# Two heads at a time in the dilated part of a decoder trunk's attention, and weight parts dealt differently over the steps

## What is computed

```
h = x @ w_in                       # (256, 3302)
# 4 heads with latent q and kv (q, k of width 96), causal softmax
# 6 forgetting heads (width 64 + 2 columns that carry the log gates), causal softmax
# 6 dilated heads, q and k rotated by position, width 64:
for window, dilation in ((128, 1), (512, 4), (2048, 16)):
    # query t sees t, t-d, ..., t-window; softmax numerators and denominators are summed over the three
    ...
mixed = concat(o_a, o_b, o_c)      # 256 + 384 + 384 = 1024
x = layer_norm(alpha * x + mixed @ w_out)
```

## Time and profile before

| | us |
|---|---|
| median of 3 runs | 868.74 |
| lowest and highest | 868.0, 871.59 |
| the profiled execution: its own time | 867.3 |
| its span, first to last instruction | 865.7 |
| TensorE busy in the span | 816.2 (94%) |
| VectorE busy | 628.9 (73%) |
| ScalarE busy | 503.0 (58%) |
| GpSimd busy | 89.9 (10%) |

### The profile page before, as it was taken

How to read it: one execution, slowest core, us unless ns; L and a number is a source line. 1 busy time by engine, 2 the same in 40 slices (tenths; PEclk the granted TensorE clock), 3 DMA queues, 4 the chain that set the end, 5 groups by cost and what they waited for, 6 DMA issues and landing times.

```text
span 865.7 us, 12257 instructions
## 1 busy us (share of the span) xinstructions
PE 816.2 (94%) x4411; PEld 695.0 (80%) x4411; DVE 628.9 (73%) x1094; ACT 503.0 (58%) x794; POOL 89.9 (10%) x165
## 2 busy tenths in 40 slices
PE   6998899899998999999999989999999989999993
PEld 6997798679876888888889978867898768888882
DVE  4656766775657899999565577666856589999984
ACT  3655554454435788888355646544443467888871
POOL 3156200030000000000020530000200100000001
PEclk9999999999999999999999999999999999999997
DMA  9953353455333699999465524425533439999941
GB/s 275 337 178 111 128 163 106 139 160 190 94 121 121 218 366 370 364 369 372 159 181 166 180 98 146 148 97 195 196 120 100 128 118 306 366 367 366 367 147 49
DMA packets 124110, 177.06 MB, mean 205 GB/s; under 512 B 12320, under 2 KB 92720, under 8 KB 124048
## 3 DMA queue, kind: packets, MB, share of 16 engines
q1 hardware_dynamic: 122064, 169.56, 58.8%
q0 software_dynamic: 1984, 6.70, 2.6%
HBM read 175.18 MB, written 1.05 MB: 204 GB/s over the span
## 4 chain that ended last, share of the span: by engine, by line
PE 81%; DVE 10%; ACT 3%; issue 3%; DMA 1%; POOL 1%; SPq 0%; DVEq 0%; ACTq 0%; POOLq 0%
PE bank L1489 21%; PE bank L1491 21%; PE bank L1490 21%; DVE w_split L490 2%; PE bank L1766 2%; PE bank L1618 2%; PE bank L1659 2%; PE bank L1607 2%; PE bank L1629 1%; PE bank L1596 1%; PE bank L1650 1%; DVE xT_lo L997 1%; DVE p_sb L1046 1%; PE bank L1606 1%; DMA xs<-in_x_dram 1%
## 5 line engine op out<-in xcount | busy, mean ns | idle before, releaser
L490 DVE TENSOR_TENSOR w_split<-raw,w_split 128x1024 fp32r<-128x1024 f32 (+2 forms) x336 | 386.9, 1174 | 74.5 <-ACT w_split L485 69.9
L485 ACT ACTIVATE w_split<-raw 128x1024 fp32r<-128x1024 f32 (+2 forms) x336 | 335.5, 1010 | 111.7 <-PE bank L1491 97.5
L1489 PE MATMUL bank<-w_split,xg_hi 128*128 128x512 f32 x256 | 103.5, 404 | 0.0
L1491 PE MATMUL bank<-w_split,xg_lo 128*128 128x512 f32 x256 | 100.2, 392 | 0.0
L1490 PE MATMUL bank<-w_split,xg_hi 128*128 128x512 f32 x256 | 100.2, 391 | 0.0
L1489 PE MATMUL bank<-w_split,xT_hi 128*128 128x384 f32 (+1 forms) x224 | 77.8, 347 | 2.0 <-DVE w_split L490 1.6
L1491 PE MATMUL bank<-w_split,xT_lo 128*128 128x384 f32 (+1 forms) x224 | 75.7, 338 | 0.0
L1490 PE MATMUL bank<-w_split,xT_hi 128*128 128x384 f32 (+1 forms) x224 | 75.6, 338 | 0.0
L602 POOL TENSOR_SCALAR st<-st 128x1 f32<-128x1 f32 x12 | 5.7, 473 | 653.4 <-ACT junk L748 653.0
L707 ACT ACTIVATE qkT<-bank 66x512 f32<-66x512 f32 (+2 forms) x32 | 19.0, 593 | 80.0 <-PE bank L1596 80.0
L1491 PEld LDWEIGHTS bank<-w_split,xg_lo 128*128 128x128 f32 x256 | 48.1, 188 | 11.0
(11 more groups left out here) (296 smaller groups left out, 1610.0 us busy)
## 6 DMA issues: line engine op xcount, KB each, us to landing
raw<-in_expert_w_gate_dram SPq DMA_DIRECT2D x128, 256.0 KB, 5.0
raw<-in_expert_w_up_dram SPq DMA_DIRECT2D x128, 256.0 KB, 6.7
raw<-in_expert_w_down_dram SPq DMA_DIRECT2D x64, 512.0 KB, 7.0
raw<-in_w_in_dram SPq DMA_DIRECT2D x48, 384.0 KB, 4.2
raw<-in_xattn_w_kv_dram SPq DMA_DIRECT2D x32, 512.0 KB, 3.7
raw<-in_w_mix_out_dram SPq DMA_DIRECT2D x16, 512.0 KB, 4.1
raw<-in_xattn_w_q_dram SPq DMA_DIRECT2D x16, 512.0 KB, 3.4
raw<-in_xattn_w_o_dram SPq DMA_DIRECT2D x16, 512.0 KB, 4.3
```

The source lines that it names most:

```text
L485: nc.scalar.activation(w_hi[:, i % SPL, 0:w], raw[:, i % RAW, 0:w], ACT.Copy).then_inc(hi_ready, 1)
L490: nc.vector.tensor_tensor(w_lo[:, i % SPL, 0:w], raw[:, i % RAW, 0:w], w_hi[:, i % SPL, 0:w].bitcast(F32), ALU.subtract).then_inc(lo_ready, 1)
L1489: nc.tensor.matmul(o, lhs[0], rhs[0], start=first, stop=False, skip_group_check=shared)
L1491: return nc.tensor.matmul(o, lhs[1], rhs[0], start=False, stop=last, skip_group_check=shared)
```

## The change

- Stream and steps: WO1 part 0 changes places with WO0 part 3, so that it comes first after step 18. `slots` deals the 29 parts anew.
- `head_qk` for heads 10, 12 and 14 transposes two heads at once (four 128x128 transposes for both), in steps 10, 12 and 14; the three odd ones fall away. It first waits until VectorE has read the previous head's scores (`s_masked`), as the odd head's scores now go into B_QK.
- `evac_qk` copies both heads with one instruction of 128 rows.
- `head_scores` runs in steps 11, 13 and 15 for two dilated heads: for each of the two token tiles first one head from rows 0 to 63, into B_S, then the other from rows 64 to 127, into B_QK. Steps 12, 14 and 16 have no scores.
- VectorE: both heads' `softmax_max` in the odd step, the first head's `softmax_norm` there too, the second's at the start of the even step. For all other heads `softmax_norm` now stands ahead of `evac_o`.

```diff
-                         ..., ("WO0", range(4)), ("WO1", range(4)),
+                         ..., ("WO0", range(3)), ("WO1", range(1)), ("WO0", range(3, 4)), ("WO1", range(1, 4)),
...
-        slots = [3] + [2] * 2 + [1] * 7 + [2] * 6 + [1] * 3
+        slots = [3, 2, 2] + [2, 1] * 4 + [1, 2] * 2 + [1] * 4
...
+        def in_pair(h):
+            return MLA_H + FOX_H <= h < HEADS
+        def qk_slot(h):
+            return (h // 2 + 1) % 2 if in_pair(h) else h % 2
...
+            return B_QK if (in_pair(h) or h >= HEADS) and (h - HEADS) % 2 else B_S
+        def scored(s):
+            if in_pair(s - 1):
+                return (s - 1, s) if s % 2 else ()
+            return (s - 1,) if 1 <= s <= HEADS else ()
...
-                nc.scalar.activation(qkT[0:d, h % 2, :], B_QK[0:d, :], ACT.Copy).then_inc(qkT_ready.sem, 1)
+                nc.scalar.activation(qkT[0:d, qk_slot(h), :], B_QK[0:d, :], ACT.Copy).then_inc(qkT_ready.sem, n)
...
-                    if 1 <= s <= HEADS:
-                        softmax_max(l, s - 1)
+                    for h in scored(s):
+                        softmax_max(l, h)
+                    if in_pair(s - 1) and s % 2 == 0:
+                        softmax_norm(l, s - 1)
                     if 2 <= s <= HEADS + 1:
                         evac_pT(l, s - 2)
+                    if 1 <= s <= HEADS and not (in_pair(s - 1) and s % 2 == 0):
+                        softmax_norm(l, s - 1)
                     if s >= 3 and (s - 3) % 2 == 1:
...
                         evac_o(l, s - 3)
-                    if 1 <= s <= HEADS:
-                        softmax_norm(l, s - 1)
...
-                if h >= MLA_H + FOX_H:
+                if in_pair(h):
+                    pe.wait_ge(s_masked.sem, s_masked.at(l, 2 * h))
                     pe.nop().then_inc(paused_t, 1)
...
+                        if in_pair(h):
+                            ins = nc.tensor.transpose(B_QK[:, c0:c0 + P], v[:, t, g:g + 2, :].rearrange("p h d -> p (h d)"),
+                                                      ident[:, :])
...
+                if in_pair(h):
+                    pe.wait_ge(qkT_ready.sem, qkT_ready.at(l, h + 2))
+                    pe.wait_ge(s_masked.sem, s_masked.at(l, 2 * h))
+                    for q, k in ((slice(0, P), slice(0, P)), (slice(P, T), slice(P, 3 * P))):
+                        for i in range(2):
+                            v = qkT[i * DIL_D:(i + 1) * DIL_D, qk_slot(h), :]
+                            ins = nc.tensor.matmul(score_bank(h + i)[:, k], v[:, q], v[:, T:T + k.stop - k.start],
+                                                   start=True, stop=True)
+                    ins.then_inc(s_done.sem, 2)
...
-                    if 1 <= s <= HEADS:
-                        head_scores(l, s - 1)
-                    if s < HEADS:
+                    if scored(s):
+                        head_scores(l, scored(s)[0])
+                    if s < HEADS and not (in_pair(s) and s % 2):
                         head_qk(l, s)
-                for i in range(index[l, "WO0", 3], index[l, "MV1", 3]):
+                for i in range(index[l, "WO1", 0], index[l, "MV1", 3]):
                     gemm(i)
```

More of the change, by code:

```diff
@@ L58, in weight_stream @@
                          ("UKV", range(1)), ("FV", range(2, 4)), ("DQ", range(4)), ("DK", range(4)), ("DV", range(4)),
-                         ("MK0", range(4)), ("MK1", range(4)), ("MV0", range(4)), ("WO0", range(4)), ("WO1", range(4)),
+                         ("MK0", range(4)), ("MK1", range(4)), ("MV0", range(4)), ("WO0", range(3)), ("WO1", range(1)), ("WO0", range(3, 4)), ("WO1", range(1, 4)),
                          ("MV1", range(4)), ("XQ0", range(4)), ("XQ1", range(4)), ("XO0", range(4)), ("XO1", range(4)),
@@ L397, in build @@
         feat = lambda w: w.rearrange("(k p) n -> p k n", p=P)
-        slots = [3] + [2] * 2 + [1] * 7 + [2] * 6 + [1] * 3
+        slots = [3, 2, 2] + [2, 1] * 4 + [1, 2] * 2 + [1] * 4
         turns, ahead_of = [], []
         for l in range(L):
-            fill = list(between(l, ("FV", 2), ("WO0", 3)))
+            fill = list(between(l, ("FV", 2), ("WO1", 0)))
             assert sum(slots) == len(fill)
@@ L409, in build @@
             assert len(turns[l]) == HEADS + 3
-            ahead_of.append(turns[l][1:] + [[index[l, "WO0", 3], index[l, "WO1", 0]]])
-        def score_bank(h):
-            return B_QK if h >= HEADS and (h - HEADS) % 2 else B_S
+            ahead_of.append(turns[l][1:] + [[index[l, "WO1", 0], index[l, "WO0", 3]]])
+        def in_pair(h):
+            return MLA_H + FOX_H <= h < HEADS
+        def qk_slot(h):
+            return (h // 2 + 1) % 2 if in_pair(h) else h % 2
+        def score_bank(h):
+            return B_QK if (in_pair(h) or h >= HEADS) and (h - HEADS) % 2 else B_S
[3 more added lines that the diff above has]
+            return (s - 1,) if 1 <= s <= HEADS else ()
         def value_bank(h):
@@ L702, in evac_qk @@
             def evac_qk(l, h):
-                act.wait_ge(qk_done.sem, qk_done.at(l, h + 1))
+                n = 2 if in_pair(h) else 1
+                act.wait_ge(qk_done.sem, qk_done.at(l, h + n))
                 if h >= 2:
                     act.wait_ge(s_done.sem, s_done.at(l, h - 1))
-                d = MLA_D if h < MLA_H else FOX_D if h < MLA_H + FOX_H else DIL_D
-                nc.scalar.activation(qkT[0:d, h % 2, :], B_QK[0:d, :], ACT.Copy).then_inc(qkT_ready.sem, 1)
+                d = MLA_D if h < MLA_H else FOX_D if h < MLA_H + FOX_H else 2 * DIL_D
+                nc.scalar.activation(qkT[0:d, qk_slot(h), :], B_QK[0:d, :], ACT.Copy).then_inc(qkT_ready.sem, n)
             def exps(l, h):
@@ L839, in _ @@
                                     .then_inc(job_a.sem, 1)
-                    if s < HEADS:
+                    if s < HEADS and not (in_pair(s) and s % 2):
                         evac_qk(l, s)
-                    if 1 <= s <= HEADS:
-                        exps(l, s - 1)
+                    for h in scored(s):
+                        exps(l, h)
                     if s >= 3 and (s - 3) % 2 == 1:
@@ L1019, in softmax_max @@
                         sl = slice(0, P) if t == 0 else slice(P, 3 * P)
-                        nc.vector.tensor_tensor_reduce(p_sb[:, h % 2, sl], B_S[:, sl], mask[:, P - P * t:2 * P], scale, -3e38,
+                        nc.vector.tensor_tensor_reduce(p_sb[:, h % 2, sl], score_bank(h)[:, sl], mask[:, P - P * t:2 * P], scale, -3e38,
                                                        ALU.add, ALU.max, mx[:, h, t:t + 1]).then_inc(s_masked.sem, 1)
```

7 lines of the change are left out of this document (4 added, 3 removed).

## The result

The changed kernel takes 845.86 us (median of 4 runs, 845.52 to 846.52), the kernel before in the same comparison 869.18 us (868.0 to 871.59). The ratio is 0.973, with an interval of 0.971 to 0.975: 23.3 us faster. The forecast was 849 us, 844 to 856. The profiled execution took 845.52 us, 21.8 less than the profiled one of before (867.3).

A forecast was written before the change was run, and what follows sets the result against it. TensorE's work and idle moments were taken as the bound. Per layer 4.0 - 1.07 + 5.3 + 1.3 = 9.5 us, 19.0 for two, gave 849.7; with small gaps the forecast was 849 us, range 844 to 856.

The forecast's parts named there:

- What bounds it: Whole kernel: TensorE, busy 94% of the span with 81% of the chain; its own work and its standing still count.
- Part 1: Dilated heads, steps 11 to 16: fewer transposes, paired scores and turns without scores save 4.0 us a layer.
- The assumption of full overlap: Steps 11, 13, 15: two heads' score matmuls run beside each other and cost what one head's do, 1.32 us with the turn.
- the serial rival: Score pairs in steps 11, 13, 15 run one after the other: +0.65 us per pair, 853 us; chance 12%.
- Part 2: Step 10: the transposes wait for head 9's mask, 1.07 us lost per layer.
- Part 3: Steps 3 to 9: five waits for softmax probabilities go, 0.4 us stays in steps 5 and 6; 5.3 us saved a layer.
- Part 4: End of the head steps: 1.5 us of waits stay, 1.5 go; 0.2 lost behind them, 1.3 us a layer net.
- The two small gaps that I left out: Parts starting 0.3 us late where GpSimd rotates, not counted in the terms: worth up to 1 us.
- The waits that come back: Softmax waits return because VectorE, with two parts to split, reaches the mask late: 857 us; chance 10%.
- No change: Head steps: waits only move and the score pairs run serially: 866.7 us; chance 3%.
- The throttle: Dilated steps: pauses bring TensorE's clock from 2.4 to 1.2 GHz, slower, 880 us if over 15 us a layer; chance 3%.

The follow-up runs named there:

- the run with the copy one step later still: Changed kernel without the wait before head 10's transposes, WO0 part 1 split in step 15, MV0's product copied in step 17: 841.52 us.
- the run head by head: Changed kernel with each pair's score matmuls ordered as both token tiles of one head, then both of the other: 846.96 us.

## Why the prediction was right

Point by point, in the terms of its sum, per layer:

- **What bounds it.** TensorE's list, by its work and by the times in which it stands still: right. Behind the head steps the change cost 0.14 us in both layers together, and the experts' stretch only shifted. TensorE's idle time fell by 13.3 us, 11 forecast; 2.1 us of it is the shorter wait for the first DMA, which isn't the change's.
- **Part 1, small work, 4.0 us.** Step 12: 0.74 us, 0.75 forecast. Step 11: 1.37, 1.32 forecast; 0.1 of it is a pause ahead of the next part that steps 13 and 15 (1.28) don't have. Two small errors cancel: the odd steps took 1.65 us before, not step 12's 1.71, so they gave 1.0 us instead of 1.17, and step 16 gave 1.0 instead of 0.93 (a turn alone is 0.30 us without a wait, in the run with the copy one step later still). The busy time fell by 8.5 us, 8.0 forecast. The assumption of full overlap is shown by the run with both heads in one half: 0.65 us more from first to last start, the 0.65 of the serial rival exactly. Its cost on the path was 1.77 us a layer, not 1.95, as it hid the pause of step 11 and 0.1 us of the wait for head 14's turn.
- **Part 2, the wait, 1.07 us lost.** The mechanism was right, the size too small: from the last score's start to the transposes it is 1.77 us in the first layer and 1.50 in the second, where 0.22 is free of a wait, so 1.55 and 1.29, 1.07 forecast. Removing it gives 1.25, as in the first layer 0.3 reappears in a split. Two things were too small. From the end of the mask to the transposes I took 0.05 us, which no row showed; it is 0.27 in both layers (first layer: mask below, transposes at 115.15). And in the first layer the mask itself ends 0.27 us later after the last score than in the kernel before, though GpSimd is idle there; why stays open.

```profile
114.46 0.42 DVE L1035 CUSTOM_DVE_ANT_0 p_sb<-bank,causal 128x256 f32<-128x256 f32 x1
```

- **Part 3, 5.3 us.** The five waits are gone; in the first layer 0.3 stayed in step 4 and 0.1 in step 5, in the second 0.5 in step 3 (forecast: 0.4 in steps 5 and 6). From start to start it is 5.3 us in the first layer.
- **Part 4, 1.5 us less at the end, 0.2 given back.** From start to start 1.8 us less. Remaining waits: 0.2 for head 14's turn, 1.0 for the split of WO0 part 1, none for part 2, where the forecast had 0.2, 1.1 and 0.2. What was given back behind the steps is 0.07, not 0.2. My reason for the split's delay, ScalarE's two heads of exponentials, was half of it: moving the split ahead of them removed that wait, but VectorE, which is full there, handed the same time to the next part.
- **The sum.** 9.5 us a layer forecast, 9.7 measured (9.8 in the head steps, 0.07 given back behind them). In the first layer, from start to start: 4.0 - 1.6 + 5.3 + 1.8, and 0.3 that my sum doesn't have. It was closer than the parts deserve, which is luck: the wait of step 10 cost 0.2 to 0.5 more, the end gave 0.4 more, and the 0.3 came on top. The two small gaps that I left out were worth less than I thought, some 0.2 us in the first layer and not up to 1 in all (0.55 us late before, in steps 3 and 6; 0.34 after, in step 5). Another 0.2 came from the turns of steps 3, 5, 7 and 9: without a stop ahead of it the turn hands over 0.06 us sooner. Step 13 took 0.1 back.
- **From 849 to 845.9.** The forecast started from the first median, 868.74, and one profiled execution. Of the 3.1 us that it lies above the result, the stretches that the change touches explain nothing: they gave 19.5 us, where the forecast had 19.0 and 0.7 more for the small gaps. 2.3 us are what the table shows outside them, start, norm and clock, which move by as much in any kernel here. The last 1.1 is that the median lay 1.4 us above the profiled execution before and 0.3 after. So of the 23.3 us between the medians only some 19.5 are the change; the run head by head, with the same head steps, is 19.7 us under the kernel before of its own comparison.

The rivals: serial pairs (853 us) are refuted by the starts and by the run in one half. The waits that come back (857 us) appear where the deal is undone: 3.4 us in steps 3 to 9, and 857.25 us. No change (866.7 us) needed both of these and is refuted with them. The throttle (slower) didn't come in the changed kernel: the head steps ran at 1.00. It does come elsewhere, in the router's stretch, with the change (0.84) and without it (0.91), and in the last head steps of the second layer in the run of the deal alone (0.93), where TensorE had been busy for 19.1 of the 20 us before (540 to 560) and for 23.0 of the 26 us of the stretch.

## What to carry to other kernels

Two products of 64 rows each cost the time of one here, with their operands in different halves of the partitions and their results in two banks (one bank for both wasn't tried); of the two orders of the list that were tried neither was better, only the place of the data counted. Where one engine's list is the path, count for every step how long the chain of the other engines is and put that much independent work in front of the instruction that waits for it; fewer dependent steps and a better deal of the filling are worth more together than apart. When a wait is taken away at a place where the helper engine has no gap, it can come back one step later, as it did here. Look at the helper's timeline, not at the list of waits, for what to move.

## What the runs showed of the hardware

- TensorE starts matmuls for different row halves beside each other even when, in the list, two matmuls of the first half stand between: starts 13 ns apart head by head, 6 to 7 ns alternately, and the same 0.93 us for the pair (if the program that ran keeps the list's order, which no trace shows). I had expected that only neighbours overlap. The Trainium skill ("TensorE: Matmul & The Clock Gate", Part 3, what overlaps and what doesn't) says that matmuls start and end in the order of the program; the starts in this trace don't follow that across halves.
- A step whose scores use 64 rows of the array takes 0.30 us longer than one whose scores use 66, with the same columns (1.71 against 1.41 us), which I read as the price of going into the narrower mode and back; four transposes of 66 columns and four of 128 (step 12 above, 126.99 to 127.35) take the same 0.36 us from the first start to the next part, so transposing two heads at once costs TensorE nothing more.
- VectorE's pieces grow while GpSimd rotates q and k. The two scalings of the probabilities take 0.55 us in one step of the kernel after and 1.79 in the next, in which GpSimd is at work; rows of VectorE, then of GpSimd:

```profile
77.31 0.55 DVE L1061 TENSOR_SCALAR p_sb<-p_sb,ri 128x128 f32<-128x128 f32 x2
...
81.83 1.79 DVE L1061 TENSOR_SCALAR p_sb<-p_sb,ri 128x128 f32<-128x128 f32 x2
...
81.48 1.02 POOL L596 TENSOR_TENSOR rot<-dk,sinb 128x384 f32<-128x384 f32 x1
82.45 1.02 POOL L597 TENSOR_TENSOR rot<-dk,cosb 128x384 f32<-128x384 f32 x1
```

  The Trainium skill ("SBUF — State Buffer", SBUF: two separate sides) calls the port pair of these two engines an exclusive lock; these rows agree, with 1.2 us lost: VectorE's pair ends at 83.62 us, right behind GpSimd's second row (83.47). With two parts in the odd steps the turn of step 5 doesn't wait for it.
